# Prompt attention inside the projection: the score and value matmuls of the two kv heads issued in turn, and other slots for the transposes and the values

## The reference

```python
def sink_attention(q, k, v, dist, valid, rel_bias, sinks):
    logits = jnp.einsum('...qhgd,...khd->...hgqk', q, k) * (HEAD_DIM ** -0.5)
    ...
    logits = jnp.where(valid, logits + bias, -jnp.inf)
    m = jnp.maximum(jnp.max(logits, axis=-1, keepdims=True), sink)
    p = jnp.exp(logits - m)
    denom = jnp.sum(p, axis=-1, keepdims=True) + jnp.exp(sink - m)
    return jnp.einsum('...hgqk,...khd->...qhgd', p / denom, v)
```

## Time and profile before

| | |
|---|---|
| time, median of 3 runs | 2617.49 us (2616.7 to 2619.95) |
| the profiled execution's own time | 2613.09 us |
| its span, first to last instruction | 2611.0 us |
| PE busy | 2428.4 us, 93% |
| DVE, ACT, POOL busy | 60%, 36%, 7% |
| share of PE in the chain that ended last | 84% |
| mean granted clock of TensorE | 0.97 |

### The profile page before, as it was taken

The page is one execution under the profiler, slowest core; times in us unless marked ns, Lnnn a source line. Parts: engine busy times, 40 slices in busy tenths (PEclk is TensorE's granted clock), DMA queues, the critical chain, the costliest instruction groups (busy, mean ns, idle before and its releaser), DMA issues.

```text
span 2611.0 us, 43931 instructions
## 1 busy us (share of the span) xinstructions
PE 2428.4 (93%) x18485; PEld 2215.3 (85%) x18485; DVE 1562.9 (60%) x2258; ACT 936.7 (36%) x1311; POOL 186.3 (7%) x212
## 2 busy tenths in 40 slices
PE   5789999999999899769999999999999989899996
PEld 1189887777777699769999999999999989899885
DVE  0332442323232332388888878888888778688788
ACT  1122331313131322254444444444444333333333
POOL 3150230000000011100000000000000000000121
PEclk8889999999999999989999999999999989999998
DMA  9954464545454333203354333443344762722622
GB/s 328 333 185 148 137 158 158 182 146 182 145 182 146 119 113 113 103 33 128 132 177 165 127 141 145 157 157 128 127 166 167 299 245 98 313 99 110 253 74 93
DMA packets 185123, 418.49 MB, mean 160 GB/s; under 512 B 13476, under 2 KB 118740, under 8 KB 181088
## 3 DMA queue, kind: packets, MB, share of 16 engines
q1 hardware_dynamic: 174720, 345.25, 38.6%
q0 software_dynamic: 7904, 65.97, 6.4%
q10 hardware_dynamic: 2304, 4.46, 0.4%
HBM read 357.65 MB, written 57.98 MB: 159 GB/s over the span
## 4 chain that ended last, share of the span: by engine, by line
PE 84%; DVE 6%; DMA 5%; issue 3%; ACT 2%; SPq 0%; POOL 0%; DVEq 0%; ACTq 0%; POOLq 0%
PE PJ L1742 25%; PE PJ L2043 24%; PE PS L2043 24%; DMA AR<-in_weights 3%; PE PJ L1695 2%; PE PS L1965 2%; DMA act_parts<-SQ 1%; PE PS L1972 1%; PE PJ L1685 1%; ACT WO L1016 1%; PE PS L1992 1%; DVE W L1503 1%; PE PS L1985 1%; DVE GR L1499 1%; DVE WO L1480 1%
## 5 line engine op out<-in xcount | busy, mean ns | idle before, releaser
L2043 PE MATMUL PJ<-HS,WO 128*128 128x272 f32 x5544 | 719.9, 292 | 76.2 <-DVE HS L1608 28.8
L2043 PEld LDWEIGHTS PJ<-HS,WO 128*128 128x128 f32 x5544 | 712.1, 191 | 80.8 <-issue 47.6
L2043 PE MATMUL PS<-HS,WO 128*128 128x272 f32 x5544 | 705.0, 288 | 5.9 <-DVE W L1503 5.1
L1480 DVE TENSOR_TENSOR WO<-GR,WO 128x1024 fp32r<-128x1024 f32 (+1 forms) x476 | 567.9, 1193 | 234.3 <-ACT WO L1016 233.6
L2043 PEld LDWEIGHTS PS<-HS,WO 128*128 128x128 f32 x5544 | 699.6, 188 | 7.9 <-DVE W L1503 6.0
L1016 ACT ACTIVATE WO<-GR 128x1024 fp32r<-128x1024 f32 (+1 forms) x476 | 490.5, 1034 | 557.7 <-DVE GR L1488 144.5
L1742 PE MATMUL PJ<-HH,WH 128*128 128x272 f32 x1632 | 365.4, 306 | 20.7 <-issue 7.9
L1742 PE MATMUL PJ<-HL,WH 128*128 128x272 f32 x1632 | 341.4, 291 | 0.0
L1742 PE MATMUL PJ<-HH,WL 128*128 128x272 f32 x1632 | 341.1, 291 | 0.0
L1742 PEld LDWEIGHTS PJ<-HH,WH 128*128 128x128 f32 x1632 | 258.1, 192 | 73.3 <-issue 61.1
L1134 DVE TENSOR_TENSOR WL<-RW,WH 128x1024 fp32r<-128x1024 f32 x102 | 126.7, 1247 | 293.1 <-ACT WH L763 292.8
(11 more groups left out here) (269 smaller groups left out, 1647.5 us busy)
## 6 DMA issues: line engine op xcount, KB each, us to landing
GR<-in_weights SPq DMA_DIRECT2D x264, 512.0 KB, 6.8
AR<-in_weights SPq DMA_DIRECT2D x256, 256.0 KB, 4.5
RW<-in_weights SPq DMA_DIRECT2D x102, 512.0 KB, 4.5
act_parts<-SQ SPq DMA_DIRECT2D x44, 952.0 KB, 7.4
AR<-in_weights SPq DMA_DIRECT2D x64, 512.0 KB, 5.4
HS<-act_parts POOLq DMA_DIRECT2D x14, 2176.0 KB, 17.0
HS<-act_parts POOLq DMA_DIRECT2D x7, 1632.0 KB, 11.6
MIX<-in_xT SPq DMA_DIRECT2D x1, 4352.0 KB, 16.8
```

The lines of the kernel that those rows point to most:

```text
L1480: d.tensor_tensor(split_part(n, 1), operand(n), split_part(n, 0).bitcast(F32), ALU.subtract)\
L2043: mm = e.matmul(out, w[part], HS[:, QUARTER[i], y, k, :], start=OPENS[i] and k == 0 and x == 0, stop=k == tiles - 1 and x == 2, skip_group ...
```

## The change

`scores` and `values` now take a pair of jobs instead of one. Inside them the loop over the kv head is innermost, so consecutive matmuls work on different halves: of the array's rows in the scores, of its output columns in the values. The two jobs wait together, and the semaphore gets one increment for each job, on the last matmul of each head. The slots change too: scores at 0 and 3 instead of 0, 1, 3, 5; transposes at 8, 9, 11, 13 instead of 8, 10, 12, 14; values at 11 and 15 instead of 10, 12, 14, 15. The other engines' programs are the same.

```diff
-        def scores(q, n):
-            job, kv, pair = 4 * q + n, n % 2, n // 2
-            rows = slice(HD * kv, HD * kv + HD)
-            if job >= 2:
-                e.wait_ge(S["att_logits"], job - 1)
+        def scores(q, pair):
+            job = 4 * q + 2 * pair
+            if job:
+                e.wait_ge(S["att_logits"], job)
             else:
                 e.wait_ge(S["dec_stored"], 2)
             for j in range(2):
                 for kb in range(1 if q == 0 else 0, 2):
-                    keys = pcol(q - 1 + kb)
-                    at = 256 * j + WIN * kb
-                    mm = e.matmul(PS[:, n % 2, at:at + WIN], MIX[rows, 2 * pair + j, pcol(q):pcol(q) + WIN],
-                                  KTT[rows, keys:keys + WIN], start=True, stop=True)
-            mm.then_inc(S["att_scores"], 1)
+                    keys, at = pcol(q - 1 + kb), 256 * j + WIN * kb
+                    for kv in range(KVH):
+                        rows = slice(HD * kv, HD * kv + HD)
+                        mm = e.matmul(PS[:, kv, at:at + WIN], MIX[rows, 2 * pair + j, pcol(q):pcol(q) + WIN],
+                                      KTT[rows, keys:keys + WIN], start=True, stop=True)
+                        if j == 1 and kb == 1:
+                            mm.then_inc(S["att_scores"], 1)
...
-        def values(q, n):
-            job, kv, pair = 4 * q + n, n % 2, n // 2
-            rows = slice(HD * kv, HD * kv + HD)
-            k0 = 1 if q == 0 else 0
-            e.wait_ge(S["att_by_key"], job + 1)
-            if n == 0 and q:
+        def values(q, pair):
+            job, k0 = 4 * q + 2 * pair, 1 if q == 0 else 0
+            e.wait_ge(S["att_by_key"], job + 2)
+            if pair == 0 and q:
                 e.wait_ge(S["att_stored"], q)
             for j in range(2):
                 for kb in range(k0, 2):
-                    mm = e.matmul(PS[rows, 3, WIN * (2 * pair + j):WIN * (2 * pair + j) + WIN], VTK[:, q - 1 + kb, rows],
-                                  PT[n % 2][:, 2 * j + kb, :], start=(kb == k0), stop=(kb == 1))
-            mm.then_inc(S["att_values"], 1)
+                    for kv in range(KVH):
+                        rows = slice(HD * kv, HD * kv + HD)
+                        mm = e.matmul(PS[rows, 3, WIN * (2 * pair + j):WIN * (2 * pair + j) + WIN],
+                                      VTK[:, q - 1 + kb, rows], PT[kv][:, 2 * j + kb, :], start=(kb == k0),
+                                      stop=(kb == 1))
+                        if j == 1 and kb == 1:
+                            mm.then_inc(S["att_values"], 1)
 
         for q in range(4):
             side = {}
-            for n in range(4):
-                for job, k in ((scores, (0, 1, 3, 5)[n]), (turn, (8, 10, 12, 14)[n]), (values, (10, 12, 14, 15)[n])):
-                    side.setdefault(k, []).append(lambda job=job, q=q, n=n: job(q, n))
+            for job, k, n in ((scores, 0, 0), (scores, 3, 1), (turn, 8, 0), (turn, 9, 1), (values, 11, 0), (turn, 11, 2),
+                              (turn, 13, 3), (values, 15, 1)):
+                side.setdefault(k, []).append(lambda job=job, q=q, n=n: job(q, n))
```

## The result

| | before | after |
|---|---|---|
| median of this comparison, 4 runs each | 2617.68 us (2616.7 to 2619.95) | 2595.68 us (2593.93 to 2600.62) |
| ratio of the times | | 0.9918 [0.9901, 0.9935] |
| the profiled execution's own time | 2613.09 us | 2593.93 us |
| its span | 2611.0 us | 2591.9 us |
| the stretch, from the first prompt scores to the first gate matmul | 116.17 us | 100.79 us |

The forecast was 2601.3 us, 2597 to 2610. The change is faster, as forecast, but the time lies 1.3 us under the range. The saving in this comparison is 22.0 us where the sum had 16.2; the stretch itself gave 15.4. So two things need a cause: why the stretch is 0.8 us off, and where the other 6.6 us come from. Later comparisons with the same two kernels gave less: the 56 later runs of before have a mean of 2613.7, the 16 later ones of after one of 2597.1.

The account below looks back on a forecast made before the run. PE's own queue was taken to bound the stretch. 18.0 us less PE work minus 1.8 of waits gave 16.2, so 2613.1 profiled became 2596.9; with the median 4.4 above, 2601.3 us, range 2597 to 2610.

Parts of the forecast that it names:

- the sum: Over the four blocks of the stretch: 18.0 us less PE work, minus 1.8 of new waits, 16.2 us saved.
- PE's queue sets the time, and what leaves it leaves the total.: In the stretch PE is busy all 26.14 us of block q = 2; work removed shortens the total unless waits replace it.
- Two at once, rows and columns.: Scores and values: matmuls on different array halves run together, 16 records in 1.08 and 1.02 us, the price of 8 before.
- the nearest row, L1695: Basis for two at once: four column quarters in turn there overlapped loads and matmuls, 32 records of 256 columns in 1.93 us.
- The clock: Granted clock 1.00 in all four blocks; the rival had it fall in each, 13.2 us lost, 2614.5, chance 0.04.
- The wait at slot 3: Second scores wait for DVE to read both first jobs: 0.45 us, at most three times, 1.4 in all.
- the transposes at slot 9: In front of L1707: 0.35 us each, plus 0.15 waiting for ACT's copy of slot 8's transposes, three times 0.45 in all.
- Block q = 0: First block of the stretch: 1.66 us from two fewer score blocks, 1.53 from values and transposes, 3.2 saved.
- One after the other, 16 x 0.11 + 0.20 = 1.96: Scores: the upper bound for 16 records if the two row halves run serially, against 1.08 us for two at once.
- both rivals built on it: Row halves serial: 2607.5 us, chance 0.14. Columns serial, 2607.5, or both, 2613.6: together chance 0.07.
- the median of the runs is 4.4 above the profiled one, so 2601.3: Last step for the whole program: 4.4 us added to the 2596.9 reached from the profiled time.
- no waits, and some noise: What the lower end of the 8-in-10 range for the total, 2597 us, allowed for.

Follow-up runs that it names:

- grouped: The changed kernel with the new slots and pairs, but one head's matmuls all issued ahead of the other's; 2603.86 us, ratio 0.9967 to before.
- before_again: The kernel of before, unedited, run against before itself; 2613.73 us, ratio 0.9997.
- again: The changed kernel once more without an edit, against before; 2598.18 us, ratio 0.9949.
- again2: The changed kernel a third time without an edit, against before; 2596.38 us, ratio 0.9939.
- again3: The changed kernel a fourth time without an edit, against before; 2595.09 us, ratio 0.9930.
- before_dec: Before with the new tokens' values reordered: all L1827 matmuls, then all L1828, heads in turn; 2604.12 us, ratio 0.9961 to before.

## Why the prediction was right in its parts and wrong in its number

**Right.** *PE's queue sets the time, and what leaves it leaves the total.* Behind the stretch both profiles take the same, 2242.3 and 2241.6 us. *Two at once, rows and columns.* 1.09 and 1.03 us for 16 records, where 1.08 and 1.02 were forecast from the earlier trace rows; the choice of the nearest row, L1695, was right. *The other pieces*: transposes 0.36 (forecast 0.35), blocks of 21.6 to 22.2 us (21.6). *The clock* stays at 1.00 in the blocks, but for the first 0.7 us of q = 0, which the fall ahead of the stretch reaches. *The wait at slot 3*: 0.43 us in q = 2 (a step from 292.81 ends at 293.56, the entry adds 0.09, the scores start at 294.08), 0.12 in q = 1 and 0.82 in q = 3. That is 1.4 in all, as forecast, but for equal shares of 0.45.

The rule of the Trainium skill (TensorE: Matmul & The Clock Gate, Part 3) that a load overlaps matmuls in flight only when its row group differs is not borne out here. The values' loads, one and the same row group, start in pairs 7 ns apart, and 16 records of 128 columns take 1.03 us.

**A term that was mis-sized: the transposes at slot 9.** The forecast was 0.35 us each and 0.15 of waiting. The timeline shows the wait in the step ahead (301.45 to 302.47 is 1.02, a step behind transposes 0.84: 0.18) and 0.47 for the transposes (302.47 to 302.94). That is 0.15 more in each of three blocks, and it accounts for q = 1 to 3: 12.6 us saved where the sum had 14.85 - 1.8 = 13.05. Block q = 0 was to give 3.2 and gave 3.1 at full clock (21.73 to 18.63). In this profile it gave 2.8, because the clock was low at its head. So the stretch is 0.8 us longer than summed, 15.4 instead of 16.2: half of that is the transposes, 0.3 the clock and 0.1 the rest of q = 0. The copy it waits for came when forecast: ACT's L860 in after, to be read against the earlier trace rows, starts 0.64 us after the transposes do, as there.

```profile
301.73 0.60 ACT L860 ACTIVATE PT<-PS 128x512 f32<-128x512 f32 x1 [3.23 <-PE PS L1865]
```

**What the turns themselves are worth.** "One after the other, 16 x 0.11 + 0.20 = 1.96" is the price if halves can't run at once, and 1.09 and 1.03 for `x16` shut that out, with both rivals built on it (6.2 us each). It is not the price of the other order: issued one head after the other, in `grouped`, a group took 1.64, since matmuls of another half start about three records early. It does not touch the forecast itself, but of the 15.7 us at full clock only 4.8 come from the turns, and 6.2 without the wait that they bring. The rest, about 11, is there in `grouped` too, which has half as many entries and exits, other slots, and the overlap of three records in each pair. No run takes these apart.

**The step that failed: "the median of the runs is 4.4 above the profiled one, so 2601.3".** It took the distance between before's median and its profiled execution as a constant that the change carries over. It isn't: after's median lies 1.75 above its profiled execution (2595.68 and 2593.93). That is 2.65 of the 5.6 us between forecast and result. The other 3.0 lie between the profiles, nearly all in pieces that the sum took as equal. In after the start is 4.0 us shorter (164.27, the shortest of the 17 profiles) and the part behind 0.7 shorter. Against that, the low clock ahead of the stretch costs 1.1 more, and the stretch itself saves 0.8 less. The first three weren't forecast, and nothing says that the change caused them: in repeats of one kernel these pieces move by 3, 2 and 1 us. They also make up the 6.6 us of the 22.0 that the stretch doesn't show: 4.0 + 0.7 - 1.1, and 2.8 between the distances of the two medians from their profiles (4.6 and 1.75).

From the profiled time alone, 2613.1 - 16.2 = 2596.9, the sum is 1.2 us off the measured 2595.68, and equal to the mean of the 20 runs of after, 2596.9. That it is so close is luck in part, since the stretch gave 0.8 less than the sum. The range had the same fault: its lower end, 2597, leaves 4.3 us under the forecast for "no waits, and some noise", where the profiled execution of before alone already lay 3.6 to 6.9 us under the three other runs of the same kernel.

The three runs shown of before, at 2617.5, were at the upper end for it; later medians are 2613.1 to 2613.9. So the saving of 22.0 in the first comparison holds 4 to 5 us that belong to that comparison's runs of before.

What goes with the level is seen in the runs. Each later run has its mean granted clock of TensorE. Of before's 56 runs with a clock those at 0.965 to 0.968 (10) have 2615.5 to 2622.1 us as means of a level, those at 0.970 (13) 2612.9, and those at 0.973 and 0.974 (8) 2611.5 and 2609.2; a line through all 56 has 1.1 us per 0.001 (r = -0.73, about half of the variance). After's 20 runs have 1.0. By an estimate, 0.001 less is 2.6 us more of the 2612 at the low level, where PE does half, so 1.3 us: near the slope. At a clock of 0.970 the lines give 2613.7 and 2597.1, 16.6 apart: close to the 16.2 of the sum. `before_again`'s profile, 6.6 us longer than before's, shows one source: 5.2 of them are the low clock in the stretch, 1.4 the start. Whether before's first runs were of this kind isn't shown: their clocks are not at hand and they were not profiled. All four lie at 2616.7 or above, where only 9 of the 56 later runs do, and the four runs of after beside them, with a mean of 2596.5, are not high. So the scatter of the later runs would rarely give it, and the cause stays open.

**The rival that something else gained**, 20 us or more wherever the change ran, fell with `again`, `again2` and `again3`: 14.9, 16.7 and 18.75 us, and with the 16.6 (15.2 to 18.0) of all later runs. The order of the new tokens' values is worth something of its own: `before_dec` is 9.8 us under before, with the stretch at 116.12 unchanged. 7.4 to 8.5 of them stand ahead of the stretch.

**Open.** What set before's first four runs high. Why the start varies by 5 us and the part behind the stretch by 8, which no kernel here takes apart; and why the clock returns sooner in one execution than in another. Whether sorted shapes alone, without the turns of the heads, would keep the clock up. Also whether the change gives a little less once the clock is up (12.2 against 16.6 us), or whether this is the scatter of five runs.

## What to carry to other kernels

Small matmuls that use half of the array are worth issuing in pairs on different halves: the pair costs what one did, and even without strict alternation a good part overlaps. Read the gain from the stretch, start to start, over a part where the granted clock is the same in both: there 12.6 us were seen to 0.05, while medians of five runs moved by 2 us and more. Give the range of the total the spread that runs of the same kernel show, in the low direction too; the distance of three runs to one profile is no constant. And look ahead of the stretch for a place where tile shapes alternate: reordering it here, shapes sorted and heads in turn together, gave 9.8 us for no work saved.

## What was not expected of the hardware

- Matmuls of the other half overtake: in `grouped` the first three records of head 1 start among the last three of head 0, ahead of program order, in scores (1.64 us against 1.96) and in values (1.52 against 1.90).
- In the alternating shapes of L1827/L1828 PE is never idle, and yet the clock falls, for 7 us in one execution of before and about 20 in another; with the shapes sorted and the heads in turn, 64 records take 2.1 us and in none of three profiles does it fall there.
- DVE's operations on two columns (L1282) take 0.16 us in most jobs, but 0.48 and 0.92 in q = 2 and 0.75 in q = 3 of after, where POOL has a large operation at the same time; the one of 0.75 us ends where POOL's L653 does (315.39 and 315.37). In all 17 profiles the 163 of them with no POOL operation beside them take 0.160 to 0.164 us, and every one over 0.2 has one; others have one and take 0.16 all the same. The wait at slot 3 grows with it, 0.12, 0.43 and 0.82 us. No run takes POOL's work away, so it is an observation only. The two rows, of DVE and of POOL:

```profile
314.64 0.75 DVE L1282 SCALAR_TENSOR_TENSOR ST<-ST,NS 128x2 f32<-128x2 f32 x1
```

```profile
314.32 1.05 POOL L653 TENSOR_TENSOR WA<-WA 128x520 f32<-128x520 f32 x1
```
